# Two modulation vectors times their matrix, on VectorE, ScalarE and GpSimd instead of TensorE, spread over the first block

## The reference, cut to what matters

```python
silu_c, silu_cc = jax.nn.silu(c), jax.nn.silu(c_ctx)
for l in range(DEPTH_2):                       # two layers
    mod = silu_c @ w_mod[l] + b_mod[l]         # 2048 x 6144 matrix
    shift, scale, gate = jnp.split(mod[:, None, :], 3, axis=-1)
    cmod = silu_cc @ w_mod[l] + b_mod[l]       # the same matrix
    cshift, cscale, cgate = jnp.split(cmod, 3)
    h = rmsnorm(x, norm_g[l]) * (1.0 + scale) + shift
    hc = rmsnorm(cx, norm_g[l]) * (1.0 + cscale) + cshift
    ...                                        # attention
    x = x + gate * (y @ w_o[l])
```

## Time and profile before

| | |
|---|---|
| median of 3 runs | 3526.9 us (3526.59 to 3531.01) |
| the profiled execution, its own time | 3526.57 us |
| its span, first to last instruction | 3524.8 us |
| TensorE (PE) busy | 3270.7 us, 93% |
| VectorE (DVE) busy | 1746.3 us, 50% |
| ScalarE (ACT) busy | 1472.7 us, 42% |
| GpSimd (POOL) busy | 224.1 us, 6% |
| mean granted clock of TensorE | 0.967 of full |
| HBM | 179 GB/s over the span |

### The profile page before, as it was taken

One profiled execution on the slowest core, in us unless ns is written; L12 is line 12 of the kernel. 1 busy time (PEld: TensorE's weight loads), 2 busy tenths in 40 slices (PEclk: granted clock), 3 DMA queues, 4 the chain that ended last, 5 costly groups with the idle time before them and its releaser, 6 DMA issues.

```text
span 3524.8 us, 39356 instructions
## 1 busy us (share of the span) xinstructions
PE 3270.7 (93%) x15208; PEld 2636.2 (75%) x15208; DVE 1746.3 (50%) x2482; ACT 1472.7 (42%) x2183; POOL 224.1 (6%) x332
## 2 busy tenths in 40 slices
PE   6999999999999999999989999999975999978767
PEld 5888888878888887888878777778754878766546
DVE  3445555556565656656563233334334345344634
ACT  3444444444464555545553233333422234344522
POOL 0000000000000000000100000000011001010010
PEclk9999999999999999999999999999986999989978
DMA  6866745466687767777753322323333325544653
GB/s 186 284 206 220 266 144 162 150 215 219 205 267 245 251 223 264 266 243 251 229 193 126 127 72 97 109 100 129 100 127 122 99 78 184 178 140 127 211 186 125
DMA packets 353237, 628.10 MB, mean 178 GB/s; under 512 B 42571, under 2 KB 109816, under 8 KB 350236
## 3 DMA queue, kind: packets, MB, share of 16 engines
q1 hardware_dynamic: 320572, 543.49, 47.5%
q0 software_dynamic: 18528, 62.93, 5.0%
q10 hardware_dynamic: 13952, 19.17, 1.6%
HBM read 579.86 MB, written 51.94 MB: 179 GB/s over the span
## 4 chain that ended last, share of the span: by engine, by line
PE 84%; DVE 6%; ACT 3%; issue 2%; DMA 2%; POOL 1%; ACTq 1%; SPq 0%; DVEq 0%; POOLq 0%
PE acc L414 25%; PE acc L419 22%; PE acc L418 22%; PE acc L1095 4%; PE acc L1122 3%; DVE w_lo L395 3%; PE acc L416 2%; PE acc L1110 2%; ACT w_hi L389 1%; PE acc L1079 1%; PE acc L743 1%; PE acc L1099 1%; ACTq L1255 1%; PE acc L651 1%; ACT stage L468 0%
## 5 line engine op out<-in xcount | busy, mean ns | idle before, releaser
L414 PE MATMUL acc<-w_hi,a_hi 128*128 128x512 f32 (+4 forms) x3800 | 1511.6, 398 | 40.4 <-issue 20.8
L395 DVE TENSOR_TENSOR w_lo<-raw,w_hi 128x1024 fp32r<-128x1024 f32 (+2 forms) x986 | 1161.0, 1208 | 749.0 <-ACT w_hi L389 731.7
L419 PE MATMUL acc<-w_hi,a_lo 128*128 128x512 f32 (+4 forms) x3800 | 1474.1, 388 | 0.0
L418 PE MATMUL acc<-w_lo,a_hi 128*128 128x512 f32 (+4 forms) x3800 | 1473.8, 388 | 0.0
L389 ACT ACTIVATE w_hi<-raw 128x1024 fp32r<-128x1024 f32 (+2 forms) x986 | 1000.5, 1044 | 744.9 <-PE acc L419 723.0
L414 PEld LDWEIGHTS acc<-w_hi,a_hi 128*128 128x128 f32 x3800 | 720.3, 190 | 206.4 <-DVE w_lo L395 38.0
L419 PEld LDWEIGHTS acc<-w_hi,a_lo 128*128 128x128 f32 x3800 | 719.1, 189 | 147.5
L418 PEld LDWEIGHTS acc<-w_lo,a_hi 128*128 128x128 f32 x3800 | 720.3, 190 | 131.5 <-issue 0.7
L1219 DVE TENSOR_REDUCE at_st<-acc 128x1 f32<-128x256 f32 (+3 forms) x208 | 101.2, 487 | 452.6 <-PE acc L1095 307.1
L1152 ACT ACTIVATE pb<-acc,at_st 128x256 f32<-128x256 f32 (+3 forms) x208 | 108.3, 521 | 382.8 <-DVE at_st L1219 359.1
L414 PE MATMUL acc<-w_hi,MV 128*128 128x512 f32 x384 | 155.9, 406 | 5.4 <-DVE w_lo L395 2.6
(11 more groups left out here) (341 smaller groups left out, 1786.5 us busy)
## 6 DMA issues: line engine op xcount, KB each, us to landing
raw<-in_w_mod SPq DMA_DIRECT2D x192, 512.0 KB, 5.2
raw<-in_w_mlp_in SPq DMA_DIRECT2D x128, 512.0 KB, 4.5
raw<-in_w_mlp_out SPq DMA_DIRECT2D x128, 512.0 KB, 5.3
raw<-in_e_w_in SPq DMA_DIRECT2D x104, 512.0 KB, 5.3
raw<-in_w_in SPq DMA_DIRECT2D x96, 512.0 KB, 4.3
raw<-in_w_in SPq DMA_DIRECT2D x88, 472.0 KB, 4.7
raw<-in_w_o SPq DMA_DIRECT2D x64, 512.0 KB, 4.8
raw<-in_o_w_in SPq DMA_DIRECT2D x64, 512.0 KB, 4.4
```

The lines of the kernel that those rows point to most:

```text
L395: nc.vector.tensor_tensor(w_lo[:, n % SPLITS, 0:size], raw[:, n % RAWS, 0:size], w_hi[:, n % SPLITS, 0:size].bitcast(F32), ALU.subtract)\
L414: nc.tensor.matmul(o, s.lhs(0, kt, tt), wh, start=kt == 0, stop=False)
L418: nc.tensor.matmul(o, s.lhs(0, kt, tt), wl, start=False, stop=False)
L419: last = nc.tensor.matmul(o, s.lhs(1, kt, tt), wh, start=False, stop=end)
```

## The change

Of the 24 steps of modulation, 20 (all of the first layer, shift and scale of the second) leave TensorE; the other four (gates of the second layer, in rest3) stay. The same matrix is now streamed in 160 chunks of 1024 columns by 128 rows (`Matvec`, 10 column blocks `j` of 16 chunks). For each chunk VectorE multiplies by the context's number of each partition and adds to a running `lanes` (one instruction), ScalarE multiplies by the token's number into `products`, and GpSimd adds that to the other `lanes`. After 16 chunks TensorE sums over partitions with 16 matmuls of one column against `ones` (`lanes_add`), and ScalarE copies the result into `mc` in SBUF (`lanes_keep`), which the layers use in place. 32 of the chunks lie in the qkv, qkv_end and gates_a stages (two for every five chunks), 32 in the branch and out1 stages and 96 in the MLP (one for every two chunks), each block of 16 followed by a gap. Nine of the setup loads move from ScalarE's queue to GpSimd's. `mod_pool` and `vec_pool` go from the place ahead of p6. The gates of the first layer are written to DRAM from `mc` during the MLP.

```diff
+        vecs = Matvec([(A["w_mod_2"][0], j * CH) for j in range(6)] + [(A["w_mod_2"][1], j * CH) for j in range(4)])
+        spots = [("qkv", i, c) for i in range(1, 10) for c in range(8)] + [("qkv_end", 0, c) for c in range(8)] + \
+                [("gates_a", i, c) for i in range(2) for c in range(8)]
+        late = [("branch", i, c) for i in range(3, 12) for c in range(4)] + \
+               [("out1", i, c) for i in range(4) for c in range(8)] + [("mlp", i, c) for i in range(28) for c in range(8)]
+        vec_spots = [spots[46 * j + 5 * i // 2] for j in range(2) for i in range(KT)] + \
+                    [late[36 * j + 2 * i] for j in range(2) for i in range(KT)] + \
+                    [late[76 + 36 * j + 2 * i] for j in range(6) for i in range(KT)]
...
-                for s_, m in zip(ins[1:], mod_steps(0, 3, 3 * it)):
-                    s_.beside(m)
-                for s_, m in zip(outs[2:], mod_steps(1, 2, 2 * it)):
-                    s_.beside(m)
...
+        def vec_add_ctx(dve, q):
+            j, k = q // KT, q % KT
+            vec_landed(dve, q)
...
+            nc.vector.scalar_tensor_tensor(out=t, in0=raw[:, vecs.raw[q] % RAWS, :], scalar=ct[:, k, 0:1],
+                                           in1=bias_row[j >= 2][:, :] if k == 0 else t, op0=ALU.mult,
+                                           op1=ALU.add).then_inc(vec_ctx, 1)
+        def vec_product(act, q):
+            vec_landed(act, q)
+            if q:
+                act.wait_ge(vec_x, q)
+            nc.scalar.activation(products[q >= 2 * KT][:, :], raw[:, vecs.raw[q] % RAWS, :], ACT.Copy,
+                                 scale=ct[:, q % KT, 1:2]).then_inc(vec_prod, 1)
+        def vec_add_x(pool, q):
+            j, k = q // KT, q % KT
+            pool.wait_ge(vec_prod, q + 1)
...
+            nc.gpsimd.tensor_tensor(t, products[j >= 2][:, :], bias_row[j >= 2][:, :] if k == 0 else t, ALU.add)              .then_inc(vec_x, 1)
+        def lanes_add(pe, j):
+            pe.wait_ge(vec_ctx, KT * (j + 1))
+            pe.wait_ge(vec_x, KT * (j + 1))
...
+            for v in range(2):
+                for n in range(CH // P):
+                    last = nc.tensor.matmul(acc[:, 4, 8 * v + n:8 * v + n + 1], lanes[j >= 2][:, v, n * P:(n + 1) * P],
+                                            ones[:, 0:1], start=True, stop=True)
...
                 if s is not None:
                     for g, c in s.order():
+                        if g is vecs:
+                            (vec_add_ctx if which == "dve" else vec_product)(eng, c)
+                            continue
...
             at2.pool(pool)
-            mod_pool(pool, 1, 1, [(4, stages["mlp"].upto["put", 4])], 0, 2 * DM)
-            vec_pool(pool, 1)
             g6_pool(pool)
```

More of the change, by code:

```diff
@@ L50, in __init__ @@
         self.chunks, self.tiles, self.lhs, self.evac = chunks, tiles, lhs, evac
-        self.width, self.wtiles, self.pair = width, wtiles, None
-    def beside(self, other):
-        self.pair = other
-        return self
-    def groups(self):
-        return [self] + ([self.pair] if self.pair else [])
+        self.width, self.wtiles, self.mods = width, wtiles, {}
     def order(self):
-        return [(g, c) for c in range(len(self.chunks)) for g in self.groups()]
+        out = []
+        for c in range(len(self.chunks)):
+            out += [(self, c)] + self.mods.get(c, [])
+        return out
 class Stage:
@@ L77, in run_hooks, with __init__, chunk @@
             f(eng)
+class Matvec:
+    def __init__(self, pieces):
+        self.pieces = pieces
+        self.raw = {}
+    def chunk(self, q):
+        W, n0 = self.pieces[q // KT]
+        return W.rearrange("(k p) n -> p k n", p=P)[:, q % KT, n0:n0 + CH]
 def count_stages(stages):
-    total = {"relu2": 1}
+    total, raw = {"relu2": 1}, []
     for st in stages:
         for s in st.steps:
-            for g in s.groups():
-                g.no, g.fill, g.put, g.done = {}, {}, {}, {}
+            s.no, s.raw, s.fill, s.put, s.done = {}, {}, {}, {}, {}
@@ new lines, in count_stages @@
+                if g is s:
+                    s.no[c] = total.get("chunk", 0)
+                    total["chunk"] = s.no[c] + 1
+                raw.append((g is s, s.no[c] if g is s else c))
+            for bank, _ in s.tiles[:-1]:
+                s.done[bank] = total.get(("done", bank), 0)
+                total[("done", bank)] = s.done[bank] + 1
+            for bank, _ in s.tiles:
+                s.fill[bank] = total.get(("fill", bank), 0)
+                total[("fill", bank)] = s.fill[bank] + 1
+                if s.evac["kind"] == "store":
+                    s.put[bank] = total.get(("put", bank), 0)
+                    total[("put", bank)] = s.put[bank] + 1
@@ L104, in count_stages @@
+            for kind in ("relu2", "branch"):
+                if s.evac["kind"] == kind:
+                    s.nth = total.get(kind, 0)
+                    total[kind] = s.nth + 1
         st.upto = dict(total)
-    return total
+    return raw
 class Unit:
@@ new lines, in vec_bias @@
+        def vec_bias(pool, j):
+            if j not in (0, 2):
+                pool.wait_ge(vec_ctx, KT * (j - 1) + 1)
+                pool.wait_ge(vec_x, KT * (j - 1) + 1)
+            else:
+                nc.gpsimd.memset(bias_row[j >= 2][:, :], 0.0).then_inc(bias_zero, 1)
+                pool.wait_ge(bias_zero, j // 2 + 1)
+            layer, c = (0, j * CH) if j < 6 else (1, (j - 6) * CH)
+            pool.dma_start(bias_row[j >= 2][0:1, :], A["b_mod_2"][layer:layer + 1, c:c + CH]).then_inc(bias_in, 16)
@@ new lines, in lanes_keep @@
+        def lanes_keep(act, j):
+            act.wait_ge(lanes_done, j + 1)
+            layer, c = (0, 8 * j) if j < 6 else (1, 8 * (j - 6))
+            nc.scalar.activation(mc[:, layer, :, c:c + 8], acc[:, 4, 0:16].rearrange("p (v n) -> p v n", v=2), ACT.Copy)\
+              .then_inc(lanes_out, 1)
+        for j, (name, i, c) in enumerate(lane_spots):
+            stages[name].hook("pe", i, c, lambda pe, j=j: lanes_add(pe, j))
+            stages[name].hook("act", i, c + 1 if c + 1 < len(stages[name].steps[i].chunks) else c,
+                              lambda act, j=j: lanes_keep(act, j))
@@ L535, in stream @@
                 if i:
-                    for g in steps[i - 1].groups():
-                        evac(eng, g)
+                    evac(eng, steps[i - 1])
                 if s is not None:
                     for g, c in s.order():
-                        if g is not s or c:
-                            split(eng, g, c)
-                        if g is s:
-                            st.run_hooks(which, i, c, eng)
-                        if c == 5 and g is s and i and steps[i - 1].evac["kind"] == "relu2":
+                        if g is vecs:
+                            (vec_add_ctx if which == "dve" else vec_product)(eng, c)
+                            continue
+                        if c:
+                            split(eng, s, c)
+                        st.run_hooks(which, i, c, eng)
+                        if c == 5 and i and steps[i - 1].evac["kind"] == "relu2":
                             hidden(eng, steps[i - 1])
@@ L1004, in evac @@
                 for s_ in self.finished(p, x):
-                    for g in s_.groups():
-                        act_evac(act, g)
+                    act_evac(act, s_)
             def pool(self, pool):
```

251 lines of the change are left out of this document (149 added, 102 removed).

## The result

The changed kernel takes 3589.65 us (median of four runs, 3587.25 to 3591.93), beside 3526.74 for the kernel before (3523.96 to 3531.01): ratio 1.0177, 95% interval 1.016 to 1.0195. It is 63 us slower, and 136 us over the forecast of 3454.

A forecast was written before the change was run, and what follows sets the result against it. TensorE, busy 93% of the span, was taken as the bound. 3526.6 - 147 - 5 - 20 - 6 + 21 + 47 + 14 + 5 + 10 + 8 = 3453.6, forecast 3454 us; 8 in 10 range 3390 to 3520.

The forecast's parts named there:

- The turns: VectorE operations with both inputs in SBUF and GpSimd's exclude each other: +47 MLP, +14 branch, +5 out1, some in qkv.
- rival A: GpSimd's additions hide in VectorE's idle time, so turns cost nothing: 3379 us, chance 0.19.
- The MLP's 47: MLP: turns outlast TensorE's time, 37 us over six blocks, plus 10 for late second chunks at steps' starts.
- In out1, 93.3 for the block against 4 x 22.9: +2: out1: a block's turns of 93.3 us against four TensorE steps; +2 us, and +3 for starts of steps.
- in all 13.0: branch: a step with two modulation chunks needs 13.0 us instead of 11.23; 8 steps, +14 us.
- Mostly hidden by the turn just counted: MLP step starts: the second chunk's delay, up to 2.35 us, was priced at 0.4 for 27 steps, 10 us.
- only moved: VectorE trades 160 low parts for multiply-adds, ScalarE 160 high parts for products; called no new work, given no cost.
- The lane sums: TensorE: 160 one-column matmuls at 0.13 us each, +21 us; 18 if 0.11 apart, 45 if 0.28.
- BROW's +8: qkv: BROW's 6 MB transfer beside the ring leaves it five chunks short; +8 us, range 0 to 15.
- B: MLP: product, addition, multiply-add and low parts form a ring, 6.9 us against TensorE's 5.44: 3572 us, chance 0.13.
- C: Start: nine loads crawl on GpSimd's queue and vector setup comes late; 15 of 20 us lost: 3469, chance 0.1.
- D: qkv: the ring starves for longer than BROW lasts, +30 us: 3484, chance 0.08.

The follow-up runs named there:

- e1: Changed kernel with 150 of GpSimd's 160 additions cut to 16 columns, token sums left out: 3474.67 us, ratio 0.9842.
- e9: Kernel before plus 112 GpSimd additions of zeros that nobody waits for, at chunks 0, 2, 4 and 6 of MLP steps: 3582.09 us, 1.0156.
- e11: Kernel before plus 112 GpSimd additions that nobody waits for, at chunks 4 to 7, the second half of MLP steps: 3543.93 us, 1.0044.
- e14: Changed kernel with 16-column additions, one lane matmul for each 16, and the gates' stores in the middle of the second attention: 3420.37 us, 0.9706.
- e7: e3 with one lane matmul of 16 columns instead of 16 of one column, lane sums left out: 3442.33 us, 0.9763.
- e4: Kernel before with only nine setup loads moved from ScalarE's queue to GpSimd's: 3507.43 us, 0.9944.
- e3: Changed kernel with both multiply-adds on VectorE, no product on ScalarE and no addition on GpSimd: 3486.44 us, 0.988.
- e12: e3 with modulation chunks placed by kind of step and the gates' stores in the middle of the second attention: 3439.48 us, 0.9752.
- e2: Changed kernel with two alternating product buffers in the MLP, so ScalarE's product no longer waits for the addition before it: 3595.05 us, 1.019.

## Why the prediction was wrong

It failed in the size of one price, in one step of accounting and in two terms, one too small and one missing. From 3454 to 3590:

- **The turns, +40.** The mechanism was as said: low parts of up to 3.43 us beside an addition, TensorE waiting for `w_lo` throughout the MLP. The price was put at 75 us more than rival A and measured 115 (e1). The MLP's 47 held, as a total: 45.7. The step that failed is the price in the stages ahead of it, 28 forecast and 74 measured. "In out1, 93.3 for the block against 4 x 22.9: +2" and branch's "in all 13.0" compare sums of VectorE's and GpSimd's work with TensorE's time and leave out what else VectorE has in such a step: in out1 two read-outs, four low parts of activations of 0.44 us and the 3.31 us for ScalarE, in branch two read-outs. A step of out1 took 29.8 us and not 23.3, one of branch 15.2 to 15.5 and not 13.0; how that divides among what was left out no run shows. In qkv an addition at each start was priced, +10, and the additions cost 25.5. That such sums are the wrong measure e9 and e11 show: the same additions cost 54 us or 15.3 by their place, with VectorE idle a fifth of the time or more in both, and by sums over a step either would be nearly free. In the MLP, too, the total hides a wrong division: an "in" step lost 3.1 us to the additions (27.4 for 24.3 in e1), an "out" step without transposes 1.3 (23.73 for 22.45), where the forecast comes to 1.8 for each (6.2 for 4.5 steps, and 0.4). "Mostly hidden by the turn just counted", 0.4 us, stands where TensorE stood 2.63 at 1099.80. That the MLP's sum was right is in part luck.
- **The clock, within those.** Gaps such as that at 1099.80 were followed by matmuls at 1.2 GHz, and the mean granted clock fell from 0.967 to 0.949. The 7600 records of the second and third matmul lines grew by 43.0 us in all against before (1495.5 + 1495.4 - 1474.1 - 1473.8); a slow one is 0.24 longer and its successor 0.20 later, so, with as much again by half for the first line, an estimate of 54 us of TensorE's time. It is contained in the 115 and in the next point. The prediction had no such term.
- **The work called "only moved", +60.** "Both are no new work, only moved" is the accounting step. With short additions and no lane sums, e14 lost 60 us against 3360: 5 at the start, 11 in qkv, 11 in branch, 9 in out1 and the first step, 28 in the MLP and a gain of 2 to 3 behind it. My reading, which no run shows by itself: the chunk is no longer in a step that VectorE shares with TensorE's extra matmuls; it stands in one whose low parts are already just in time.
- **The lane sums, +23.** 44 us (e7) for 21. The nearest row, a transpose's weight load, was of another kind: 32 instructions for 16. The upper bound of 45 held it.
- **The stores of the gates, +12 to 13.** The forecast has no term for them, neither for GpSimd nor for what they do to the ring.

75 + 40 + 60 + 23 + 12 on A's 3379 gives 3589; the 60 is what e14 leaves over, so the sum tests only that the others add up. What held: the start (-15 in the trace, -20 in the medians of e4), p6 (its first square sum, over at 2702.44, is followed by GpSimd at 2702.53, and all behind the MLP gains 7.8 us for 6, in e1, e3, e14 and e12 7 to 9), the price of the matmuls taken away (the last two steps of the MLP, which hold nothing of modulation now, take 21.76 us each for 28.41 and 30.05: 0.233 for each of 64 matmuls), and BROW's +8 (the step of qkv under it took 28.39 us for 21.08, and 30.54 in e14). Of the rivals, B gave the right side and nearly the right time with a link, ScalarE's product, that e2 showed to be none; C and D don't say where the time went. What would show it ("a pass of the MLP of about 200 us", by B 228) reads 209.5, 209.9 and 224.3 for the three passes from read-out to read-out, the last with the two stores in it.

Not settled: how the 60 us divide between VectorE's order of work, ScalarE's products and the ring's raw places, which hold one chunk in three for modulation. No run varied the number of places or took the products alone away. Two steps hint that more than one counts: an "in" step takes 24.3 us in e14, with the product on ScalarE, and 23.2 in e7, without; an "out" step 22.45 and 23.66.

## What to carry to other kernels

A helper engine that excludes the one it relieves was no relief here: VectorE with all the work (3486) beat VectorE with half of it (3590). Price an added operation at the place in the step with the least in hand, with everything else that its engine has and waits for there, not by sums over a block, and look for the place where it is free; placement alone, of the chunks and of two stores, gave another 47 us. Count a small transfer by its pieces and by the ring it runs beside, and ask of each matmul of full float32 how often it stands in the trace.
